# The opening of a two-block transformer kernel: one weight slot on a second DMA queue, the other slots ahead of x's second quarter, and splits that alternate with scaled copies

## The reference

```python
def rmsnorm(x, g):
    y = x * rsqrt(mean(x * x, axis=-1) + EPS)
    return y * g

def swiglu(x, w_gu, w_down):
    gate, up = split(x @ w_gu, 2)          # w_gu: 1024 x 5632
    return (silu(gate) * up) @ w_down      # w_down: 2816 x 1024

h = x + 0.5 * swiglu(rmsnorm(x, ffn1_norm), ffn1_w_gu, ffn1_w_down)
```

## Time and profile before

| | |
|---|---|
| median of three runs | 996.52 us |
| profiled execution, its own time | 996.54 us |
| its span, first to last instruction | 994.7 us |
| TensorE busy | 989.1 us |
| VectorE busy | 682.8 us |
| ScalarE busy | 551.0 us |
| GpSimd busy | 115.5 us |
| HBM read | 182.45 MB |

### The profile page before, as it was taken

How to read it: one execution, slowest core, us unless ns; L and a number is a source line. 1 busy time by engine, 2 the same in 40 slices (tenths; PEclk the granted TensorE clock), 3 DMA queues, 4 the chain that set the end, 5 groups by cost and what they waited for, 6 DMA issues and landing times.

```text
span 994.7 us, 12552 instructions
## 1 busy us (share of the span) xinstructions
PE 989.1 (99%) x4616; PEld 811.6 (82%) x4616; DVE 682.8 (69%) x997; ACT 551.0 (55%) x760; POOL 115.5 (12%) x109
## 2 busy tenths in 40 slices
PE   8999999999999999999999999999999999999998
PEld 6788888888877788888888887888888888888887
DVE  5766566668987667656565678776689767656663
ACT  7444443576766546444443586868885555443542
POOL 0000000022300000000000041169904000000000
PEclk9999999999999999999999999999999999999999
DMA  8987776585444446766666486658555546787761
GB/s 260 286 262 255 236 252 211 188 305 175 147 150 143 169 131 213 227 201 211 213 203 222 159 246 219 171 168 212 150 190 195 205 156 205 231 219 226 226 197 43
DMA packets 163353, 200.92 MB, mean 202 GB/s; under 512 B 53857, under 2 KB 109546, under 8 KB 163178
## 3 DMA queue, kind: packets, MB, share of 16 engines
q1 hardware_dynamic: 162714, 200.16, 63.6%
q10 hardware_dynamic: 592, 0.14, 0.1%
HBM read 182.45 MB, written 5.77 MB: 189 GB/s over the span
## 4 chain that ended last, share of the span: by engine, by line
PE 96%; DMA 1%; DVE 1%; POOL 0%; ACT 0%; SPq 0%; issue 0%; ACTq 0%; DVEq 0%
PE bank L1941 23%; PE bank L1943 23%; PE bank L1942 23%; PE bank L2057 7%; PE bank L2059 7%; PE bank L2058 7%; PE bank L1956 1%; PE bank L2108 1%; PE bank L2222 1%; DMA rg<-rg 1%; DMA raw<-in_ffn_w_gu 1%; PE bank L2123 0%; PE bank L2110 0%; PE bank L2180 0%; DVE lo L1323 0%; PE bank L2345 0%
## 5 line engine op out<-in xcount | busy, mean ns | idle before, releaser
L1941 PE MATMUL bank<-hi,xh 128*128 128x512 f32 (+1 forms) x944 | 375.0, 397 | 0.9 <-DVE lo L1549 0.8
L1943 PE MATMUL bank<-hi,xl 128*128 128x512 f32 (+1 forms) x944 | 367.3, 389 | 0.0
L1942 PE MATMUL bank<-lo,xh 128*128 128x512 f32 (+1 forms) x944 | 366.5, 388 | 0.0
L1306 DVE TENSOR_TENSOR lo<-raw,hi 128x2048 fp32r<-128x2048 f32 (+1 forms) x111 | 253.9, 2289 | 146.5 <-ACT hi L815 146.5
L815 ACT ACTIVATE hi<-raw 128x2048 fp32r<-128x2048 f32 (+1 forms) x114 | 216.5, 1901 | 133.1 <-PE bank L2059 96.9
L1941 PEld LDWEIGHTS bank<-hi,xh 128*128 128x128 f32 x944 | 177.3, 188 | 39.6 <-issue 2.7
L1943 PEld LDWEIGHTS bank<-hi,xl 128*128 128x128 f32 x944 | 177.1, 188 | 37.4
L1942 PEld LDWEIGHTS bank<-lo,xh 128*128 128x128 f32 x944 | 177.5, 188 | 34.4
L1323 DVE TENSOR_TENSOR lo<-raw,hi 128x1024 fp32r<-128x1024 f32 (+1 forms) x108 | 132.2, 1234 | 42.3 <-ACT hi L824 41.7
L2057 PE MATMUL bank<-hi,hh 128*128 128x512 f32 (+1 forms) x306 | 119.3, 390 | 0.0
L2059 PE MATMUL bank<-hi,hl 128*128 128x512 f32 (+1 forms) x306 | 118.7, 388 | 0.0
(11 more groups left out here) (269 smaller groups left out, 957.5 us busy)
## 6 DMA issues: line engine op xcount, KB each, us to landing
raw<-in_w_in SPq DMA_DIRECT2D x48, 1024.0 KB
raw<-in_ffn_w_gu SPq DMA_DIRECT2D x82, 512.0 KB
raw<-in_ffn_w_down SPq DMA_DIRECT2D x22, 1024.0 KB
raw<-in_w_up SPq DMA_DIRECT2D x16, 1024.0 KB
raw<-in_w_down SPq DMA_DIRECT2D x16, 1024.0 KB
raw<-in_w_out SPq DMA_DIRECT2D x8, 1024.0 KB
distance_table<-ftab SPq DMA_DIRECT2D x8, 576.0 KB
raw<-in_w_proj_attn SPq DMA_DIRECT2D x4, 1024.0 KB
```

The source lines that it names most:

```text
L1306: nc.vector.tensor_tensor(lo[s][:, :, 0:width], raw[s][:, :, 0:width], hi[s][:, :, 0:width].bitcast(F32), ALU.subtract).then_inc(lo_done, 1)
L1941: nc.tensor.matmul(o, sh, wh, start=first and j == 0, stop=False)
L1942: nc.tensor.matmul(o, sh, wl, start=False, stop=False)
L1943: ins = nc.tensor.matmul(o, sl, wh, start=False, stop=last and j == 3)
```

## The change

SyncE's order becomes quarter 0, slots 0.1 to 0.3, quarter 1, slot 1.0, quarter 2, slots 1.1 and 1.2, quarter 3, slot 1.3. Slot 0.0 is loaded by ScalarE's queue, ahead of the gains. On ScalarE the splits of unit 0 alternate with the scaled copies of the first quarter, slot first; the squares of the first quarter go to VectorE, as one multiply with a running sum, and those of the second quarter move behind unit 1's splits. On VectorE the same alternation follows. On TensorE the second quarter's transposes move from behind group 0 to behind group 1, and three identity transposes instead of eight follow the first quarter's.

```diff
+        def slot_view(n, j):
+            view = a["ffn1_w_gu"].rearrange("(k p) (g f c) -> k f p g c", p=P, g=2, c=GU)
+            return view[4 * (n % 2) + j, n // 2]
 # SyncE
             quarter(0)
-            slot(0, 0)
-            slot(0, 1)
+            for j in range(1, 4):
+                slot(0, j)
             quarter(1)
-            for j in range(2, 4):
-                slot(0, j)
+            slot(1, 0)
             quarter(2)
-            slot(1, 0)
+            slot(1, 1)
+            slot(1, 2)
             quarter(3)
-            for j in range(1, 4):
-                slot(1, j)
+            slot(1, 3)
 # ScalarE
+            act.dma_start(raw[0][:, 0, :].rearrange("p (g c) -> p g c", g=2),
+                          slot_view(0, 0)).then_inc(slot_in[0][0], 16)
             act.dma_start(crow0[:, :], a["ffn1_norm"].rearrange("a (n c) -> (a n) c", c=P)).then_inc(gain0_in, 16)
...
-            half_squares(0)
+            slot_hi(0, 0)
             act.wait_ge(gain0_done, 1)
-            first_turned_hi(0, 0)
-            slot_hi(0, 0)
-            for j in range(1, 4):
+            for j in range(4):
                 first_turned_hi(0, j)
-            slot_hi(0, 1)
-            half_squares(1)
-            slot_hi(0, 2)
-            slot_hi(0, 3)
+                if j < 3:
+                    slot_hi(0, j + 1)
...
             for j in range(1, 4):
                 slot_hi(1, j)
+            half_squares(1)
             for j in range(4):
                 first_turned_hi(3, j)
 # VectorE
-            first_turned_lo(0, 0)
-            slot_lo(0, 0)
-            for j in range(1, 4):
+            dve.wait_ge(x_in[0], 16)
+            nc.vector.tensor_tensor_reduce(xn[:, 0, 0:W], resid[:, 0, 0:W], resid[:, 0, 0:W], 1.0, 0.0, ALU.mult, ALU.add,
+                                           ss_left[:, 0:1]).then_inc(n_left, 1)
+            for j in range(4):
+                slot_lo(0, j)
                 first_turned_lo(0, j)
-            for j in range(1, 4):
-                slot_lo(0, j)
 # TensorE: behind_first is now behind_second
-                    if j == 0 and behind_first is not None:
-                        behind_first()
+                    if j == 1 and behind_second is not None:
+                        behind_second()
...
             turn_norm(0, 0)
-            warm(8)
+            warm(3)
```

More of the change, by code:

```diff
@@ L552, in slot @@
             def slot(n, j):
-                src = a["ffn1_w_gu"].rearrange("(k p) (g f c) -> k f p g c", p=P, g=2, c=GU)[4 * (n % 2) + j, n // 2]
-                ins = sp_eng.dma_start(raw[n][:, j, :].rearrange("p (g c) -> p g c", g=2), src)
+                ins = sp_eng.dma_start(raw[n][:, j, :].rearrange("p (g c) -> p g c", g=2), slot_view(n, j))
                 if n == 2:
@@ L1914, in use, with portion @@
                 pe.wait_ge(lo_done, n + 1 + RING * off)
-            def portion(n, t, dst, st_hi, st_lo, kt0, first, last, width=W, behind_first=None):
+            def portion(n, t, dst, st_hi, st_lo, kt0, first, last, width=W, behind_second=None):
                 rows = slice(t * P, (t + 1) * P)
@@ L1988, in very_first @@
                     ins = portion(u, t, G[t], xh, xl, 4 * u, u == 0, u == 1,
-                                  behind_first=(lambda: turn_norm(0, 1)) if k == 0 else None)
+                                  behind_second=(lambda: turn_norm(0, 1)) if k == 0 else None)
                     if t == 1:
```

## The result

The changed kernel takes 998.97 us (median of 12 runs, 997.56 to 1001.24) against 996.59 us for the kernel before in the same job (12 runs, 996.14 to 997.06). The ratio is 1.0025, 95% interval 1.0018 to 1.0032: slower by 2.4 us, outside the range of 995.2 to 997.3. The profiled execution took 998.26 us, 1.72 us more than the one before.

What follows compares the result with a forecast made beforehand. TensorE was taken as the bound, busy 989.1 of 994.7 us, with only the opening to win. The opening's steps summed to 0.3 us gained at 20.56 us: 996.54 - 0.3 = 996.2 us, range 995.2 to 997.3.

Steps and rivals of the forecast that it cites:

- no further wait of TensorE beyond the 0.3 us in the earlier trace, whose own chain starts from TensorE: Behind the opening: only the known 0.3 us wait at the query transposes remains, so nothing is added to the sum.
- 1.1 us freed in front of the first product: Opening, TensorE: five fewer identity transposes free 1.1 us; the remaining ones end near 6.3 us, in nobody's way.
- rival 3: Opening: TensorE's clock stays at the low level longer; 1.7 us late, 998.2 us, 2.4 us at worst; chance 0.10.
- a new wait behind 24 us: Sign that the prediction is wrong altogether: TensorE shows a new wait later than 24 us.
- Gains: ScalarE's queue: gains behind slot 0.0 land at 4.3 us (3.7 to 5.5); TensorE stands about 0.5 us for them.
- the gains' transpose after 5 us: Sign that the prediction is wrong altogether: TensorE transposes the gains later than 5 us.
- Squares on VectorE: Opening: first quarter's squares take VectorE 0.75 us (0.43 to 0.85), where it idled before; ScalarE loses 0.63 us of work.
- First product: Opening, TensorE: first product at 6.75 us, before at 6.88.
- Second quarter: Opening: x's second quarter lands at 8.75 us (7.5 to 9.6), TensorE waits 0.3 us; next transposes 0.45 us ahead.
- rival 1: Opening: the second queue fills early DMA holes, second quarter at 8.2 us; gain 0.8 to 1.0, 995.6 us; chance 0.20.
- Second half: Opening to 20.56 us: ScalarE's squares put the fourth quarter's scaled copies at 14.8 instead of 15.12; TensorE resumes at 20.26, 0.3 ahead.
- over 1 us for the second quarter's transposes: Sign of rival 3: the four transposes of x's second quarter take over 1 us.

Runs made afterwards that it cites:

- kernel 2: Changed kernel with eight identity transposes instead of three behind the first quarter's; 997.51 us, ratio 1.0006.
- kernel 13: Changed kernel with TensorE's order eight identity transposes, x's first quarter, four more, the gains' transpose, eight more; 996.31 us, ratio 0.9997.
- kernel 6: Changed kernel with slot 0.0 back on SyncE's queue, the gains first on ScalarE's, and eight identity transposes; 997.27 us, ratio 1.0011.
- the kernels of the table: Kernels with the change's queues and splits, differing in where identity and gains' transposes stand, beside the kernel before; their medians 996.29 to 997.51 us.
- 5: Changed kernel with thirteen identity transposes instead of eight ahead of the gains, three still behind the first quarter's; 996.33 us, ratio 0.9998.
- kernel 12: Changed kernel with TensorE's order eight identity transposes, x's first quarter, four more, the gains' transpose, four more; 996.29 us, ratio 1.0001.
- kernel 3: Kernel before with three identity transposes instead of eight behind the first quarter's, nothing else; 998.92 us, ratio 1.0026.
- 4: Changed kernel with the gains' DMA ahead of slot 0.0's on ScalarE's queue; 999.90 us, ratio 1.0034.
- 10: Changed kernel: gains' transpose behind x's first quarter, one identity transpose ahead of it, three behind, four at the first hidden tile's wait; 997.34 us, ratio 1.0007.

## Why the prediction was wrong

**The step that failed** is "no further wait of TensorE beyond the 0.3 us in the earlier trace rows, whose own chain starts from TensorE". The sum took the five removed transposes as 1.1 us freed in front of the first product and, apart from the clock of rival 3, as nothing else. Their removal also moved the instruction load from 582.7 to 593.0 us and made that wait 1.8 us: 1.5 us in the profiled execution, and 1.5 to 2.4 us between the median of kernel 2 and the two medians of the changed kernel. The wait was in the list of waits beforehand. Its chain was taken to move along with TensorE, from which it starts; but its longest piece is a DMA of 6.38 us, with TensorE standing at its end. That chain shows that the 0.3 us grows one for one with anything that holds the transposes up; that an instruction load would do so, no row of the prediction could show. The prediction's sign for it, a new wait behind 24 us, appeared.

**The opening's steps.**

- *Gains.* Predicted at 4.3 us (3.7 to 5.5); they landed at 5.07, 3.65 us from their issue. The value was mis-sized, the bounds held (in kernel 13 the gains came at 5.76, beyond them). TensorE stood 1.34 us, where "about 0.5" was said. The prediction's sign for this, the gains' transpose after 5 us, appeared.
- *Squares on VectorE.* Predicted 0.75 us, hidden; 0.68 and 0.08 for the read, hidden behind x's transposes. Right.
- *First product.* 6.75 predicted, 7.34 measured: the gains' delay, passed on by the scaled copies. With the slow clock on top, TensorE came to the second quarter's transposes only at 9.49 instead of 8.75, so x's DMA, on which the forecast let this stretch hang, was not waited for at all.
- *Second quarter.* 8.75 predicted, 7.78 measured, and 7.78 to 8.58 in the ten profiles with the second queue: around the 8.2 of rival 1, whose gain of 0.8 to 1.0 us did not come with it. More was moved early than before (312 GB/s in the fourth microsecond against 218, 365 against 321 in the fifth), but kernel 6 moved 272 with one queue. The Trainium skill, "DMA: Bandwidth & Descriptors", section "Issuing engines are not separate DMA queues", says that a second issuer only saves issue time. Against kernel 6, whose quarter landed at 9.38, the ten came 0.8 to 1.6 us earlier, and 0.65 us of that is the earlier issue (3.26 instead of 3.91); the 0.15 to 0.95 us that are left are of the size by which the ten differ among themselves (0.8), so these runs neither bear the rule out nor contradict it.
- *Second half.* The next transposes came at 11.30, not 10.8; ScalarE's squares stood ahead of the last scaled copies as predicted, these started at 15.21 instead of 14.8, and TensorE resumed at 20.64 instead of 20.26. The twelfth transfer landed at 12.11, predicted 13.5, without effect: ScalarE made unit 1's last three high parts from 12.96 on, behind the third quarter's scaled copies, which had waited for the transposes of 11.30. With the clock early (13), though the gains still came at 5.76, the opening gains nothing either: 20.56.

**Rival 3, the clock,** was right in mechanism and got too small a chance, 0.10; its price of 1.7 us is above the 0.6 to 1.5 us measured at the next chunk's start in the kernels of the table. Its sign, over 1 us for the second quarter's transposes, appeared in the second profile of the changed kernel (1.04 us) and not in the first. That the median of 998.97 us lies near its 998.2 is chance: 1.5 us of the loss are the far wait. The prediction said that TensorE had work "from 1.8 to 6.3 with one gap" and counted that against the rival; by 2, 5 and 13 the gap was the point. In the profile shown first, the products are at the fast level from 8.79 us, close to the "beyond about 8" from which it was to decide, and only 0.08 us were lost. The Trainium skill, "TensorE: Matmul & The Clock Gate", section "Part 1: The HAM clock gate", has sustained activity release the full clock: the kernels with long stops agree. But kernel 12 was busy until 6.73 us and came to full clock only at 11.09, and the changed kernel, with fast products from 8.79 us in one profile and full clock from 10.97 in the other, shows that the moment differs from run to run.

**No version is faster.** Kernel 13 keeps the change and is without both losses: 996.31 us, ratio 0.9997 (0.9988 to 1.0006), no difference from before that these runs can tell. The gain forecast for the opening, 0.3 us, could not have been told apart either.

## What to carry to other kernels

A wait of 0.3 us behind a DMA chain without slack is a place to watch: follow its chain back before calling an edit free, even one that lies 580 us away. Instructions that compute nothing still hold two things in place here, the clock in front of the first real work and the points at which instructions are loaded; after an edit to them compare the list of waits over the whole span and not only at the edit. Where two otherwise equal runs differ by about a microsecond, look at the durations of the first products before looking for a wait.

## What the runs showed that was not expected

- With one 16 KB instruction load (0.96 us) among DMA transposes of packets under 512 B, the DMA engines were next to idle for 1.4 us; the same load at 582.7 us (0.97 us), at the end of a large transfer, cost nothing that shows.
- The load's place jumps: 582.7 us with eight and with six identity transposes, 592.6 with three.
- In one and the same program the clock rises at different times: the changed kernel has fast products from 8.79 us in one profile and full clock from 10.97 us in the other, and its next chunk starts at 20.64 and 21.66. The two groups of kernel 12 (8 and 3 of 11 runs, 1.4 us apart) fit that; only a late run of it was profiled.
- In ten runs (changed kernel one and three, kernel 3 two, 4 one, 6 two, 10 one) the mean granted clock is 0.998, and in none of the kernel before for which it is on record (114). All but the one of kernel 4 are 0.75 to 2.4 us above the median of their kernel's other runs. No profile is of such a run, so where in the span the clock was low is open.
